# The rounded weights' buffers of feed-forward and gates start 128 bytes later

## The chip, the cores and the metric

The kernel runs on one core of one Trainium2 chip. The metric is the time of one execution on the device, in microseconds (us); lower is better. The core has four engines that compute: TensorE (PE in the rows; its weight loads are PEld), VectorE (DVE), ScalarE (ACT) and GpSimd (POOL). SP, the sync engine, issues most DMAs. An engine's work is in its own order; between engines, semaphores set the order.

## What is computed

512 tokens of width 1024 pass through two blocks in float32. The first has a Hyena mixer, neighbourhood attention, a pooling mixer and 16 experts of a mixture with a choice by the experts. The second has a gated delta rule and an mLSTM, and ends as follows; the change is in the memory that this end uses:

```python
mixed = jax.nn.sigmoid(gate_a) * y_a + jax.nn.sigmoid(gate_b) * y_b
x = x + mixed @ w_out
h = _rmsnorm(x, g_ffn)
x = x + (jax.nn.silu(h @ w1) * (h @ w3)) @ w2          # 1024 -> 2816 -> 1024
gate = jax.nn.sigmoid(_rmsnorm(x, g_ple) @ w_ple_gate)  # 1024 -> 1024
x = x + gate * (p_i @ w_ple)
return _rmsnorm(x, g_final)
```

## The kernel before

**Memory.** One tensor, the arena, holds 53200 words of 4 bytes in each of the 128 partitions. Places are given in words: `view(start, ...)` is a float32 view of it, and `rounded(name, start, n)` a tensor of the type fp32r laid over the same place. The ring of weight slots begins at word 11024: four slots (R) of 2048 words (WCH). B is 19216, T0 is 39696. Where a sentence says "slot i", it is `view(11024 + 2048 * i)`.

**Products in three parts.** A float32 product is made of three in fp32r: an operand is split into a rounded part (hi) and what rounding left (lo), and lo x hi, hi x lo and hi x hi are summed in PSUM. For weights this takes three steps: SP loads a chunk of 1 MB (128 x 2048 words) into a slot; ScalarE copies it, rounded, into `whi[i]` (lines 1773, 1808, 1819, 128x2048 each); VectorE subtracts that from the slot and writes the rest back over the slot itself, as `wlo[i]` (lines 1420, 1466, 1487). Then TensorE may read both. `whi[i]` is `weight_rounded{i}` in the rows, `wlo[i]` is `weight_rest`.

**The stages that use whi.** They are the last three, and TensorE runs them in this order:

- the up half of the feed-forward: 22 chunks, two for each pair of column tiles (w1 and w3), `up_tile`, lines 962 to 964. Of its three products for each of 8 steps, 962 has wlo as the stationary operand, 963 and 964 have whi. Each streams 512 columns of the tokens. In a row of TensorE the moving operand is named first and the stationary one second.
- the down half: 12 chunks, lines 993 to 995. Here the weights are the moving operand of 512 columns; 993 and 995 read whi. The hidden values' rounded part is made by ScalarE (line 1805), their rest by VectorE (line 1462), in the order 4 rests of hidden values, then the chunk's rest.
- the gates: 4 chunks, lines 1022 to 1024, in the same form; 1022 and 1024 read whi.

A slot is loaded anew when the products of the chunk four before have been made. Between the products TensorE turns tiles with an identity (line 548 for the norms' inputs, line 972 for the scale of the rows).

Before these, the projection units (lines 601 to 603) and the branch products (lines 929 to 931) work in the same way with other buffers for the rounded part: `unit_rounded` and `branch_rounded`. The two branch buffers lie at words 33552 and 35600 (lines 1724 and 1376 are their copy and difference).

**Places before.** whi[i] is at T0 + 4096 + 2048 i, that is word 43792 + 2048 i. The four end at T0 + 12288, where `junk` of 1024 words begins: squares for the norms are written there and never read; only their sum is used (lines 521, 1839, 1853, 1862).

Of the kernel before, what the change touches and what calls it, by code (L numbers as in the profile page):

```python
# [14 lines left out]
D = 1024  # L15
# [29 lines left out]
R = 4  # L45
LOW = 16
WCH = 2048
# [115 lines left out]
def program(nc, A, out):  # L163
    ctx = ExitStack()
    with ctx:
# [20 lines left out]
        def view(start, *dims):  # L186
            n = int(np.prod(dims))
            v = arena[:, start:start + n]
            if len(dims) == 2:
                v = v.rearrange("p (a b) -> p a b", b=dims[1])  # L190
            elif len(dims) == 3:
                v = v.rearrange("p (a b c) -> p a b c", b=dims[1], c=dims[2])
            return v

        def rounded(name, start, n):

            return nc.alloc_sbuf_tensor_at(name, [P, n], F32R, offset=arena_at + 4 * start)[:, :]
# [184 lines left out]
        T0 = B + 20480  # L382
# [41 lines left out]

        junk = view(T0 + 12288, D)
        blk = grow[:, 0:7 * P].rearrange("p (l c) -> p l c", c=P)
        maT = view(T0, 4, 512)
        atT = view(T0 + 2048, 4, 512)  # L430
# [44 lines left out]
        def qkv_unit(u):  # L475

            return u if u < U_GATES else u + 1
        whi = [rounded(f"weight_rounded{i}", T0 + 4096 + WCH * i, WCH) for i in range(R)]


        ahi = [rounded(f"hidden_rounded{k}", B + 512 * k if k < 8 else B + 13312 + 512 * k, L) for k in range(NFT)]
# [2960 lines left out]
```

How the kernel before makes its waits and increments, by code:

```python
            def wait(self, n=None):  # L399
                self.eng.wait_ge(S(self.name), self.n if n is None else n)
# [21 lines left out]
        def wait_chunk(pe, c):  # L422
            pe.wait_ge(S(f"chunk_in{c % R}"), 16 * (c // R + 1))
# [93 lines left out]
        def norm_square(act, norm, i, ready, n):  # L517
            act.wait_ge(S(ready), nth(ready, n))
            act.wait_ge(S("norm_sq"), NT * norm + i)
            act.activation(junk, x_res[:, i, :], ACT.Square, accum_out=nstat[norm][:, i:i + 1]).then_inc(S("norm_sq"), 1)
# [1 line left out]
        def norm_root(act, norm):  # L523
            act.wait_ge(S("norm_var"), NT * (norm + 1))
            act.activation(nstat[norm], nstat[norm], ACT.Sqrt).then_inc(S("norm_sd"), NT)
# [1 line left out]
        def norm_scales(dve, norm):  # L527
            dve.wait_ge(S("norm_sq"), NT * (norm + 1))
            dve.tensor_scalar(nstat[norm], nstat[norm], 1.0 / D, EPS, ALU.mult, ALU.add).then_inc(S("norm_var"), NT)
            dve.wait_ge(S("norm_sd"), NT * (norm + 1))
            dve.reciprocal(nstat[norm], nstat[norm]).then_inc(S("r_made"), 1)
# [1 line left out]
        def norm_var(dve, norm, i):  # L534
            dve.wait_ge(S("norm_sq"), NT * norm + i + 1)
            v = nstat[norm][:, i:i + 1]
            dve.tensor_scalar(v, v, 1.0 / D, EPS, ALU.mult, ALU.add).then_inc(S("norm_var"), 1)
# [1 line left out]
        def norm_rstd(dve, own, norm, i):  # L539
            dve.wait_ge(S("norm_sd"), NT * norm + i + 1)
            v = nstat[norm][:, i:i + 1]
            own(dve.reciprocal(v, v))
            own.wait()
```

## Time and profile before

| | us |
|---|---|
| median of 3 runs | 2056.72 |
| lowest and highest run | 2054.0, 2059.84 |
| span of the profiled execution | 2052.9 |
| TensorE busy in it | 1952.2 |
| VectorE busy | 730.4 |
| ScalarE busy | 532.1 |
| GpSimd busy | 118.6 |

The span runs from the first to the last instruction of one execution that the hardware profiler took. Busy time of TensorE is that of pipelined products: two overlap, so the duration of one is longer than the step from one start to the next, and the step is what the stage pays. The page's second part gives TensorE's granted clock as a share of its full 2.4 GHz; the lower level is half of it.

### The profile page before, as it was taken

To read this page: it belongs to the slowest core of one execution; us is meant where nothing else is said; L and a number is where in the kernel's file an instruction comes from. 1 tells how busy PE (TensorE), PEld (TensorE's weight loads), DVE (VectorE), ACT (ScalarE), POOL (GpSimd) and SP (SyncE) were. 2 spreads that over 40 slices of the span, in tenths; PEclk is the share of its full clock that TensorE was granted. 3 is DMA by queue.
4 is the path that set the end of the run, shared out by engine and by line. 5 is a ranking of instruction groups with operands and counts; after the bars stand their busy time and mean duration, and the time that the engine had idled before them with its cause. 6 is when DMAs were issued, how large, how long until landed. Compare 5 with 4: busy or idle time off the path is not lost.

```text
span 2052.9 us, 22852 instructions
## 1 busy us (share of the span) xinstructions
PE 1952.2 (95%) x9422; PEld 1211.6 (59%) x9422; DVE 730.4 (36%) x1069; ACT 532.1 (26%) x828; POOL 118.6 (6%) x127
## 2 busy tenths in 40 slices
PE   8999999989899897989899899999999999999998
PEld 6867843333333332323333368878888888888886
DVE  5648331101001010100101067595588443345225
ACT  5236220101000000101000056334444332234125
POOL 3432000000000000000000000141000000000000
PEclk9999999999999999999999999999999999999999
DMA  9420789999999999999999933212114222323331
GB/s 273 144 72 18 297 342 430 427 431 429 431 430 432 432 430 427 432 430 429 431 434 425 423 128 134 82 43 83 62 62 146 101 83 82 119 85 113 109 140 59
DMA packets 42295, 517.33 MB, mean 252 GB/s; under 512 B 5216, under 2 KB 5344, under 8 KB 12656
## 3 DMA queue, kind: packets, MB, share of 16 engines
q1 hardware_dynamic: 39728, 508.39, 60.6%
q0 software_dynamic: 2496, 7.92, 1.8%
q8 instruction: 53, 0.87, 0.2%
q14 instruction: 18, 0.15, 0.0%
HBM read 508.92 MB, written 6.29 MB: 251 GB/s over the span
## 4 chain that ended last, share of the span: by engine, by line
PE 73%; DMA 20%; DVE 5%; ACT 1%; issue 1%; POOL 0%; SPq 0%; ACTq 0%; DVEq 0%
DMA arena<-in_w_gu_dram 19%; PE bank L2517 15%; PE bank L2542 6%; PE bank L964 4%; PE bank L963 4%; PE bank L962 4%; PE bank L601 3%; PE bank L602 3%; PE bank L603 3%; PE bank L2479 2%; PE bank L994 2%; PE bank L993 2%; PE bank L995 2%; PE bank L2143 2%; PE bank L2149 2%; PE bank L2145 2%
## 5 line engine op out<-in xcount | busy, mean ns | idle before, releaser
L2517 PE MATMUL bank<-arena 128*64 128x512 f32 x2048 | 480.3, 625 | 67.8 <-DMA arena<-in_w_gu_dram 63.9
L2517 PEld LDWEIGHTS bank<-arena 128*64 128x64 f32 x2048 | 163.1, 143 | 360.2 <-issue 348.0
L3014 DVE TENSOR_TENSOR arena<-arena,bank 128x256 f32<-128x256 f32 x64 | 27.0, 421 | 639.6 <-ACT arena L3255 639.6
L2542 PE MATMUL bank<-arena 128*64 128x512 f32 x1024 | 232.6, 595 | 0.6 <-ACT arena L3259 0.6
L3255 ACT ACTIVATE arena<-bank 128x256 f32<-128x256 f32 x64 | 24.6, 384 | 537.0 <-PE bank L2517 537.0
L2542 PEld LDWEIGHTS bank<-arena 128*64 128x64 f32 x1024 | 73.7, 137 | 139.2 <-issue 139.2
L962 PE MATMUL bank<-input_rounded,weight_rest 128*128 128x512 f32 x352 | 137.2, 390 | 0.0
L964 PE MATMUL bank<-input_rounded,weight_rounded 128*128 128x512 f32 x352 | 137.0, 389 | 0.0
L963 PE MATMUL bank<-input_rest,weight_rounded 128*128 128x512 f32 x352 | 137.0, 389 | 0.0
L601 PE MATMUL bank<-input_rounded,weight_rest 128*128 128x512 f32 x312 | 125.9, 403 | 1.2 <-DVE weight_rest L1050 1.2
L603 PE MATMUL bank<-input_rounded,unit_rounded 128*128 128x512 f32 x312 | 122.4, 392 | 0.0
L602 PE MATMUL bank<-mix_rest,unit_rounded 128*128 128x512 f32 x312 | 122.3, 392 | 0.0
L3259 ACT ACTIVATE arena<-bank 128x256 f32<-128x256 f32 x64 | 24.6, 384 | 214.9 <-PE bank L2528 214.9
L963 PEld LDWEIGHTS bank<-input_rest,weight_rounded 128*128 128x128 f32 x352 | 66.1, 188 | 13.8
L962 PEld LDWEIGHTS bank<-input_rounded,weight_rest 128*128 128x128 f32 x352 | 66.1, 188 | 13.7
L964 PEld LDWEIGHTS bank<-input_rounded,weight_rounded 128*128 128x128 f32 x352 | 66.1, 188 | 13.6
L1420 DVE TENSOR_TENSOR weight_rest<-arena,weight_rounded 128x2048 fp32r<-128x2048 f32 x22 | 50.3, 2291 | 52.1 <-ACT weight_rounded L1773 51.9
L993 PE MATMUL bank<-weight_rounded,hidden_rest 128*128 128x512 f32 x176 | 68.8, 391 | 0.0
L995 PE MATMUL bank<-weight_rounded,hidden_rounded 128*128 128x512 f32 x176 | 68.5, 389 | 0.0
L994 PE MATMUL bank<-weight_rest,hidden_rounded 128*128 128x512 f32 x176 | 68.5, 389 | 0.0
L1553 ACT ACTIVATE unit_rounded<-arena 128x1024 fp32r<-128x1024 f32 x45 | 47.3, 1059 | 79.4 <-PE bank L603 63.8
L601 PEld LDWEIGHTS bank<-input_rounded,weight_rest 128*128 128x128 f32 x312 | 59.1, 189 | 14.7 <-DVE weight_rest L1050 1.6
(528 smaller groups left out, 2851.1 us busy)
## 6 DMA issues: line engine op xcount, KB each, us to landing
arena<-in_w_gu_dram SPq DMA_DIRECT2D x47, 4096.0 KB, 28.9
arena<-in_w_d_dram SPq DMA_DIRECT2D x62, 2048.0 KB, 26.5
arena<-in_wpack_dram SPq DMA_DIRECT2D x83, 1024.0 KB, 5.0
arena<-in_w_gu_dram SPq DMA_DIRECT2D x32, 2048.0 KB, 17.4
arena<-in_w_d_dram SPq DMA_DIRECT2D x4, 1024.0 KB, 10.0
arena<-in_w_gu_dram SPq DMA_DIRECT2D x3, 1024.0 KB, 8.3
arena<-in_xT_dram SPq DMA_DIRECT2D x4, 512.0 KB, 7.2
arena<-in_x_dram SPq DMA_DIRECT2D x2, 1024.0 KB, 13.2
```

The costliest lines, as they stand in the source:

```text
L601: mm(b, wl[:, k, :], hhi[k], start=k == 0, stop=False)
L602: mm(b, wh[:, k, :], chlo[k], start=False, stop=False)
L603: last = mm(b, wh[:, k, :], hhi[k], start=False, stop=k == KD - 1)
L962: mm(b, wl[:, k, m], hhi[k], start=k == 0, stop=False)
L963: mm(b, wh[:, k, m], hlo[k], start=False, stop=False)
L964: last = mm(b, wh[:, k, m], hhi[k], start=False, stop=k == KD - 1)
L993: mm(b, alo[k][:, t], wh[:, k - 4 * d, :], start=k == 0, stop=False)
L994: mm(b, ahi[k][:, t], wl[:, k - 4 * d, :], start=False, stop=False)
L995: last = mm(b, ahi[k][:, t], wh[:, k - 4 * d, :], start=False, stop=k == NFT - 1)
L1420: tt(out=wlo[(c + which) % R], in0=w, in1=whi[(c + which) % R], op=ALU.subtract)\
L2517: last = mm(ab[64 * x:64 * x + 64, :], xsT[:, k, 64 * x:64 * x + 64], w[x][k], start=k == 0, stop=k == KD - 1)
L2542: last = mm(bank[4 + n][64 * x:64 * x + 64, :], hidT[c % 2][:, P * t + 64 * x:P * t + 64 * x + 64], w[:, x, t, 512 * n:512 * n + 512], sta ...
```

## The change

The four buffers of rounded weights and the junk behind them start 32 words, 128 bytes, later. Sizes, instructions, waits and their order are as before. The 32 words ahead of whi[0] are used by nothing in these stages.

```diff
-        junk = view(T0 + 12288, D)
+        junk = view(T0 + 12288 + 32, D)
...
-        whi = [rounded(f"weight_rounded{i}", T0 + 4096 + WCH * i, WCH) for i in range(R)]
+        whi = [rounded(f"weight_rounded{i}", T0 + 4096 + 32 + WCH * i, WCH) for i in range(R)]
```

## Rows read from the trace of the kernel before

**Rows 1.** The page's head and its line of busy times.

```profile
span 2052.9 us, 22852 instructions
PE 1952.2 (95%) x9422; PEld 1211.6 (59%) x9422; DVE 730.4 (36%) x1069; ACT 532.1 (26%) x828; POOL 118.6 (6%) x127
```

**Rows 2.** Windows: from:to, length, busy us (count) of each engine, clock, DMA.

```profile
1637.00:2044.00 407.00, 407.00 (x1815) 336.96 (x1813) 168.00 (x171) 137.99 (x142) 0.00 (x0) 1.00 0.27 99
2044.00:2052.90 8.90, 0.00 (x0) 0.00 (x0) 4.32 (x10) 3.79 (x7) 1.40 (x1) 0.65 0.32 118
```

**Rows 3.** Timeline of PE, start and duration in us: up stage, then branch stage.

```profile
1701.98 0.39 PE L964 MATMUL bank<-input_rounded,weight_rounded 128*128 128x512 f32 x1
...
1705.38 0.39 PE L964 MATMUL bank<-input_rounded,weight_rounded 128*128 128x512 f32 x1
...
1600.05 0.39 PE L931 MATMUL bank<-branch_rounded,mixed_rounded 128*128 128x512 f32 x1
...
1603.45 0.39 PE L931 MATMUL bank<-branch_rounded,mixed_rounded 128*128 128x512 f32 x1
```

**Rows 4.** Timeline of PE behind a group of transposes in the up stage.

```profile
1648.01 0.60 PE L972 MATMUL bank<-arena 128*128 128x128 f32 x4
1648.36 0.48 PE L962 MATMUL bank<-input_rounded,weight_rest 128*128 128x512 f32 x1
1648.68 0.39 PE L963 MATMUL bank<-input_rest,weight_rounded 128*128 128x512 f32 x1
```

**Rows 5.** Chain that ended last: start, us, what; one piece of 16 transposes.

```profile
1969.61 1.75 PE bank L548 x16
```

**Rows 6.** Instructions by line: durations min/median/max in ns, first and last start.

```profile
L1773 ACT ACTIVATE weight_rounded<-arena x22: 1897/1918/1924, 1613.2 to 1841.1; 128x2048 fp32r<-128x2048 f32 x22
L1808 ACT ACTIVATE weight_rounded<-arena x12: 1905/1917/1926, 1860.3 to 1963.6; 128x2048 fp32r<-128x2048 f32 x12
L1420 DVE TENSOR_TENSOR weight_rest<-arena,weight_rounded x22: 2283/2292/2293, 1615.5 to 1843.1; 128x2048 fp32r<-128x2048 f32 x22
L1466 DVE TENSOR_TENSOR weight_rest<-arena,weight_rounded x12: 2281/2292/2294, 1862.3 to 1965.6; 128x2048 fp32r<-128x2048 f32 x12
L1724 ACT ACTIVATE branch_rounded<-arena x8: 1902/1917/1923, 1538.8 to 1611.4; 128x2048 fp32r<-128x2048 f32 x8
L1376 DVE TENSOR_TENSOR weight_rest<-arena,branch_rounded x8: 2286/2292/2293, 1540.8 to 1613.3; 128x2048 fp32r<-128x2048 f32 x8
```

**Rows 7.** Instructions by line, two others of VectorE.

```profile
L2692 DVE TENSOR_TENSOR arena<-bank,arena x2: 691/692/692, 99.7 to 105.1; 128x512 f32<-128x512 f32 x2
L2641 DVE TENSOR_TENSOR weight_rest<-arena,first_weight x20: 1215/1220/2104, 15.6 to 108.0; 128x1024 fp32r<-128x1024 f32 x20
```

**Rows 8.** Timeline at the second down chunk: its rest, its first product.

```profile
1880.91 2.29 DVE L1466 TENSOR_TENSOR weight_rest<-arena,weight_rounded 128x2048 fp32r<-128x2048 f32 x1
...
1887.84 0.39 PE L993 MATMUL bank<-weight_rounded,hidden_rest 128*128 128x512 f32 x1
```

**Rows 9.** The page's groups: count, then busy us, mean ns, idle before.

```profile
L962 PE MATMUL bank<-input_rounded,weight_rest 128*128 128x512 f32 x352 | 137.2, 390 | 0.0
L964 PE MATMUL bank<-input_rounded,weight_rounded 128*128 128x512 f32 x352 | 137.0, 389 | 0.0
L963 PE MATMUL bank<-input_rest,weight_rounded 128*128 128x512 f32 x352 | 137.0, 389 | 0.0
L601 PE MATMUL bank<-input_rounded,weight_rest 128*128 128x512 f32 x312 | 125.9, 403 | 1.2 <-DVE weight_rest L1050 1.2
L603 PE MATMUL bank<-input_rounded,unit_rounded 128*128 128x512 f32 x312 | 122.4, 392 | 0.0
L602 PE MATMUL bank<-mix_rest,unit_rounded 128*128 128x512 f32 x312 | 122.3, 392 | 0.0
...
L963 PEld LDWEIGHTS bank<-input_rest,weight_rounded 128*128 128x128 f32 x352 | 66.1, 188 | 13.8
```

**Rows 10.** Instructions by line: the tail's square into junk.

```profile
L1853 ACT ACTIVATE arena<-arena x1: 629/629/629, 2046.2 to 2046.2; 128x512 f32<-128x512 f32 x1
```

## The prediction

> **What bounds the kernel now.** Read the page first: one core, a span of 2052.9 us, TensorE busy for 95% of it [rows 1]. The edit touches only the end of the kernel, so the next view is the busy time of each engine in the stretch from 1637.0 us, where the first product with a moved buffer starts, to 2044.0 us, where the last one starts, and in the tail behind it [rows 2]. In the stretch TensorE is busy for 407.00 of 407.00 us at a granted clock of 1.00, its upper level of 2.4 GHz; VectorE has 168.00 us of work there, ScalarE 137.99, GpSimd none. TensorE alone is the bound.
>
> How close is it to its own floor? The timeline gives starts: line 964 at 1701.98 and again, 15 products later, at 1705.38, so 3.40 / 15 = 226.7 ns from one 128x128 by 512-column product to the next [rows 3]. The stretch has 22 x 2 x 3 x 8 = 1056 such products of the feed-forward's up half, 4 x 22 x 2 x 3 = 528 of the down half, and 8 x 8 x 3 = 192 of the gates: 1776. 1776 x 226.7 ns = 402.6 us. The other 36 instructions of the stretch's 1815 (three more began just before it) are transposes: 4 of line 972 and 32 of line 548. Sixteen of those take 1.75 us, 0.109 each [rows 5], so 36 take 3.9. They stand in six groups, and behind a group the pipe refills: the first product after line 972 starts at 1648.36 and the next at 1648.68, 0.32 us in place of 0.227, so some 0.1 us for each group, 0.6 in all [rows 4]. 402.6 + 3.9 + 0.6 = 407.1, against 407.0. Nothing is left over but rounding; I allow 1 us for what such a sum can hide.
>
> **The change part by part.** It adds, removes and reorders no instruction, wait or DMA; it changes start addresses. Four buffers of 8 KiB per partition (whi) and the throw-away output of the squares (junk) move up by 128 bytes. No instruction before 1613 us reads or writes them. Who touches them:
>
> (1) ScalarE writes whi from a ring slot: 38 copies of 128x2048. The median is 1918 or 1917 ns, from 1897 to 1926 in lines 1773 and 1808 [rows 6]. (2) VectorE reads slot and whi and writes the difference back over the slot: 38 of 2291 ns or so, between 2281 and 2294 in lines 1420 and 1466 [rows 6]. (3) TensorE reads whi in two of every three products: 704 + 352 + 128 = 1184, in the up half as the stationary operand, in the down half and the gates as the moving one. (4) ScalarE's squares write junk, one half-width square of them in the tail.
>
> Slot i and whi[i] lie 32768 words, exactly 128 KiB, apart now. If that distance cost something, another distance should be cheaper. The trace has one: the branch weights are rounded into buffers that start 88 KiB behind slot 0, so at other multiples of 8 KiB from their slots. The same copy takes 1917 there and the same difference 2292 ns (medians of lines 1724 and 1376) [rows 6]. So (1) and (2) have no penalty to lose that depends on this distance. For a step of 128 bytes itself the trace has no twin. The nearest are the two products of line 2692, on VectorE, which write 512 elements into rows 2176 bytes apart (an odd multiple of 128), at 691 and 692 ns, one like the other [rows 7]. I take zero for (1) and (2).
>
> What if it isn't zero? Both hide under TensorE, and the tightest place sets the cover. VectorE starts the rest of the second down chunk at 1880.91 and ends it 2.29 us later, at 1883.20; TensorE first reads it at 1887.84 [rows 8]. That leaves 4.6 us. The slowest that any such difference got in this trace is 2104 ns where 1215 is the least (line 2641) [rows 7]: a factor of 1.73, which would add 1.67 us to a 2.29 us difference. Even so TensorE wouldn't wait. In the other direction, a faster copy or difference ends earlier before the same 4.6 us, and buys nothing: ring slots come free by TensorE's products, not by VectorE.
>
> (3) is the only part on the path. 226.7 ns at 2.4 GHz are 544 cycles for 512 columns. If the 32 extra cycles came from reading whi beside the other operand, they should be missing where other buffers are read. They aren't: the branch stage has line 931 at 1600.05 and, 15 products on, at 1603.45, 226.7 ns again [rows 3]. That stage keeps its rounded weights at another place in the memory and at another distance from the stationary operand. I take zero for (3). Bounds: below, at most the 1 us above; above, the worst neighbour that I have, the projection units, where the three products have a mean of (125.9 + 122.4 + 122.3) / 936 = 395.9 ns where the up half has (137.2 + 137.0 + 137.0) / 1056 = 389.4 [rows 9]. That is 6.5 ns, true waits included, and is too high by those.
>
> (4) The tail's square of 512 elements is 629 ns [rows 10], on ScalarE, and sits beside or on the last chain. A change of a few per cent is 0.02 us. Zero.
>
> Sum: 0 on the path. The profiled span is 2052.9 us and the three runs have a median of 2056.72, 3.8 more, which I keep as what lies around the span. Forecast **2056.7 us**.
>
> Here a rule of the Trainium skill bears on the upper bound. The trace shows the copies, with DMA and other engines at work beside them, within 1897 to 1926 ns, which is not one fixed number [rows 6]. SBUF — State Buffer, section "Who interferes with whom", says that only the port pair shared by VectorE and GpSimd causes contention, and that TensorE and ScalarE never wait on anyone. By that the slower rival below is impossible and its time is that of the forecast; by the rows it stays open, with a small chance. The same page's section on the DMA port swizzle speaks against an effect of any such shift too: it puts the cost in 16-byte lines, of which 128 bytes are eight whole ones. No row here shows a line's cost.
>
> **The rivals.** (A) *The copies and differences change, hidden.* ScalarE or VectorE rows of whi move by tens of ns or more. For it: nothing but that the exact 128 KiB is gone. Against: the equal rows at another distance [rows 6]. Time the same, 2056.7, by the 4.6 us of cover.
>
> (B) *Slower: TensorE's read of whi.* Place: the 1184 products that read it. A new start makes the weight load or the moving stream meet another stream of reads or writes at the same place of the memory, and the product gets longer. Price: at the 6.5 ns of the units, 1184 x 6.5 = 7.7 us, so 2064.4. It decides above 0.3% (6.2 us), so from 6.2 / 1184 = 5.2 ns a product, 2.3% of 226.7. Against it: some 70 of the copies and differences run beside the stretch's products, and the sum for it leaves nothing over; weight loads are 188 ns of the 226.7 [rows 9] and so have 39 ns of room of their own.
>
> (C) *Faster: the 32 cycles are a conflict after all*, and go with the shift. 512 columns at 2.4 GHz would be 213.3 ns (estimate: one column a cycle), 13.4 less, x 1184 = 15.8 us, so 2040.9. Against: the same 226.7 in a stage that doesn't touch whi [rows 3].
>
> (D) *The change does nothing it says*, since where a tile starts has no part in any of these durations. That isn't apart in time from the forecast.
>
> **How the numbers follow.** About 0.3%, 6.2 us, is what a measurement of this kernel can tell from no change. Forecast (with D) 0.81, A 0.10, B 0.05, C 0.04. So within 0.3%: 0.91; slower by more: 0.05; faster by more: 0.04. The forecast's own spread isn't from the sum, whose end below is 1 us, but from one run to the next: the three runs span 2054.0 to 2059.84, 3 us to each side. I take 2052.5 to 2061.0, a little wider for another session. It leaves out B and C, and with the forecast's own tails some 0.15.
>
> **What would show it.** In the changed kernel's profile: line 964 to line 964 fifteen products on, 3.40 us; the stretch from the first line 962 to the last line 1024, 407 us; the copies of lines 1773 and 1808 at 1917 and the differences of 1420 and 1466 at 2292 ns. A differs in these copies only; B and C show as a start-to-start step away from 226.7 ns in lines 962 to 964, 993 to 995 and 1022 to 1024 and not in line 931. A span that moved with none of these means a difference outside the edit, in the 1637 us before it. The prediction is wrong if a step of 128 bytes matters where steps of 4 KiB and 8 KiB don't: that is the one thing that the rows can't exclude.

## The result and the profile after

| | before | after |
|---|---|---|
| median, us | 2058.41 (5 runs) | 2065.78 (5 runs) |
| lowest and highest, us | 2054.0, 2059.84 | 2062.47, 2066.5 |
| span of the profiled execution, us | 2052.9 | 2064.0 |

The ratio is 1.0039, 95% interval 1.0028 to 1.0050: slower by about 8 us. The forecast was no change, with a range that ended at 2061.0; both were wrong.

Where do the 8 us go? The first view is that of the three stages again, by windows from the first product of each stage to the first of the next (the last ends at the start of the last product). Columns as in rows 2. Before:

```profile
1637.01:1876.96 239.95, 239.95 (x1063) 198.71 (x1062) 96.62 (x96) 77.08 (x71) 0.00 (x0) 1.00 0.25 94
1876.96:1999.70 122.74, 122.74 (x557) 101.90 (x556) 49.09 (x45) 36.04 (x36) 0.00 (x0) 1.00 0.36 129
1999.70:2043.61 43.91, 43.91 (x199) 36.34 (x197) 21.90 (x31) 24.86 (x36) 0.00 (x0) 1.00 0.14 49
```

After:

```profile
1639.66:1886.55 246.89, 246.89 (x1063) 198.79 (x1062) 96.68 (x96) 77.20 (x71) 0.00 (x0) 1.00 0.25 91
1886.55:2010.46 123.91, 123.91 (x558) 101.83 (x556) 49.10 (x45) 35.87 (x36) 0.00 (x0) 1.00 0.36 128
2010.46:2054.73 44.27, 44.27 (x199) 36.30 (x197) 22.07 (x31) 24.85 (x36) 0.00 (x0) 1.00 0.13 48
```

Same counts, same clock of 1.00, the same work of VectorE and ScalarE, TensorE busy from end to end, and longer: up by 6.94 us, down by 1.17, gates by 0.36, together 406.60 to 415.07, that is 8.47 us. 8.47 / 2057 is 0.41%, beside 0.39% measured (0.28 to 0.50). The spans differ by 11.1, and the 2.65 us more are the later start of the first up product (1639.66 in place of 1637.01). Nothing moved is used by TensorE before that point, and in the runs below that leave the earlier stages as they were it starts anywhere from 1635.9 to 1640.8 us, whatever their time. I take it for the spread of one execution.

Next the timeline of TensorE in the up half of the changed kernel (start, duration in us), as in rows 3:

```profile
1700.12 0.40 PE L964 MATMUL bank<-input_rounded,weight_rounded 128*128 128x512 f32 x1
1700.35 0.40 PE L962 MATMUL bank<-input_rounded,weight_rest 128*128 128x512 f32 x1
1700.59 0.39 PE L963 MATMUL bank<-input_rest,weight_rounded 128*128 128x512 f32 x1
1700.82 0.40 PE L964 MATMUL bank<-input_rounded,weight_rounded 128*128 128x512 f32 x1
...
1703.62 0.40 PE L964 MATMUL bank<-input_rounded,weight_rounded 128*128 128x512 f32 x1
```

From 1700.12 to 1703.62 are 15 products: 3.50 / 15 = 233.3 ns where it was 226.7 [rows 3]. All three lines are slow. The step behind 962 is 235 ns, behind 963 and 964 about 232.5. Of the stage's 350 triples that I could time, 344 take 0.700 us, so the copies of ScalarE, which run beside some of them, make no difference. In the down half the step behind 993 is the long one (232.4); behind 994 it is 226.2, behind 995 228.4 (means over the stage's starts in the timeline; before, each line's mean was 226.4 to 227.0 in the two halves). The branch stage isn't touched: line 931 starts at 1602.69 and, 15 products on, at 1606.10, 3.41 us.

What the prediction expected of the other engines holds. The copy and the difference are as in rows 6 (min/median/max ns):

```profile
L1773 ACT ACTIVATE weight_rounded<-arena x22: 1898/1917/1922, 1615.8 to 1849.3; 128x2048 fp32r<-128x2048 f32 x22
L1420 DVE TENSOR_TENSOR weight_rest<-arena,weight_rounded x22: 2284/2293/2295, 1618.2 to 1851.3; 128x2048 fp32r<-128x2048 f32 x22
```

And the page says which of TensorE's two kinds of instruction got longer:

```profile
L962 PE MATMUL bank<-input_rounded,weight_rest 128*128 128x512 f32 x352 | 140.0, 398 | 0.0
L964 PE MATMUL bank<-input_rounded,weight_rounded 128*128 128x512 f32 x352 | 139.0, 395 | 0.0
L963 PE MATMUL bank<-input_rest,weight_rounded 128*128 128x512 f32 x352 | 138.3, 393 | 0.0
...
L963 PEld LDWEIGHTS bank<-input_rest,weight_rounded 128*128 128x128 f32 x352 | 66.2, 188 | 15.6
```

Against rows 9 the products went from 389 or 390 ns to 393 to 398; the weight loads stayed at 188. Which load runs beside which product, the timeline of the loads shows:

```profile
1700.35 0.19 PEld L963 LDWEIGHTS bank<-input_rest,weight_rounded 128*128 128x128 f32 x1
1700.59 0.19 PEld L964 LDWEIGHTS bank<-input_rounded,weight_rounded 128*128 128x128 f32 x1
```

Line 962's product starts at 1700.35 too, and 963's at 1700.59: beside each product the weights of the next one are loaded.

### The profile page after: what moved, and what is told of

It reads as the page before. It is cut to its first block, busy times and chain, and to the rows that moved or that the text cites. A ratio compares the mean times of both kernels' runs of the same rounds, so it can differ in the third digit from the quotient of the medians.

```text
span 2064.0 us, 22852 instructions
## 1 busy us (share of the span) xinstructions
PE 1962.6 (95%) x9422; PEld 1214.4 (59%) x9422; DVE 730.4 (35%) x1069; ACT 531.9 (26%) x828; POOL 117.9 (6%) x127
## 4 chain that ended last, share of the span: by engine, by line
PE 72%; DMA 21%; DVE 5%; ACT 1%; issue 1%; SPq 0%; ACTq 0%; DVEq 0%
DMA arena<-in_w_gu_dram 20%; PE bank L2517 14%; PE bank L2542 6%; PE bank L962 4%; PE bank L964 4%; PE bank L963 4%; PE bank L601 3%; PE bank L602 3%; PE bank L603 3%; PE bank L2479 2%; PE bank L993 2%; PE bank L995 2%; PE bank L994 2%; PE bank L2143 1%; PE bank L2149 1%; PE bank L2145 1%
## 5 line engine op out<-in xcount | busy, mean ns | idle before, releaser
L2542 PE MATMUL bank<-arena 128*64 128x512 f32 x1024 | 232.5, 595 | 0.6 <-ACT arena L3259 0.6
L1420 DVE TENSOR_TENSOR weight_rest<-arena,weight_rounded 128x2048 fp32r<-128x2048 f32 x22 | 50.3, 2292 | 51.3 <-ACT weight_rounded L1773 51.1
```

What stands on the lines that cost most here:

```text
L1420: tt(out=wlo[(c + which) % R], in0=w, in1=whi[(c + which) % R], op=ALU.subtract)\
L2542: last = mm(bank[4 + n][64 * x:64 * x + 64, :], hidT[c % 2][:, P * t + 64 * x:P * t + 64 * x + 64], w[:, x, t, 512 * n:512 * n + 512], sta ...
```

## The experiments

The theory from here on: TensorE reads the moving operand of one product while it loads stationary weights for a product, and the two reads get in each other's way unless their operands start at the same place modulo some small stride (R). The rivals: ScalarE's and VectorE's accesses to whi are in the way (M); the place of whi in itself counts, its alignment (A); the distance between the two weight tiles wlo and whi counts (W). A step is the time from one start to the next; where one number stands for a stage, it is the mean. Single runs of a kernel differ by some 6 us (before: 2054.0 to 2059.84), so one run's time says little here. The lengths of the three stages say more: in three kernels that cost nothing they agree within 0.01 us.

**One shift for each buffer.** Buffer i serves each fourth chunk, so one kernel holds four shifts.

```diff
-whi = [rounded(f"weight_rounded{i}", T0 + 4096 + WCH * i, WCH) for i in range(R)]
+whi = [rounded(f"weight_rounded{i}", T0 + 4096 + [8, 16, 64, 128][i] + WCH * i, WCH) for i in range(R)]
```

(junk follows the last one, here and in all kernels below.)

> The four buffers of rounded weights begin 32, 64, 256 and 512 bytes later than before (8, 16, 64, 128 words), one shift for each buffer. In the changed kernel the up half's products came at 233.3 ns (three in 700 ns) where they had come at 226.7, and the first of the down half's three at 232.5. Theory R (relation): the cost depends on the distance between whi and another operand of TensorE, modulo some small stride. Then chunks in whi[0] to whi[3] have different steps, and those of the whole stride (512 bytes at the latest, since blocks of one tile lie 512 bytes apart and all cost the same before) are back at 226.7. Theory M (memory, other engines): ScalarE's and VectorE's accesses to whi disturb TensorE at any place but the old one: steps above 226.7 and irregular in time for all four. I expect 226.7 for whi[3] and 230 to 235 for at least two of the others.

> Shifts of 128, 384, 640 and 768 bytes (32, 96, 160, 192 words). whi[0] repeats the changed kernel: 233.3 ns in the up half, 232.5 for the first of three in the down half. Theory R with a stride of 512 bytes: whi[2] (640 = 512 + 128) equals whi[0]; with a stride of 256 bytes, whi[3] (768) is back at 226.7 too and whi[1] (384) equals whi[0]. Theory M: all four alike.

Single runs: 2062.53 and 2062.59 us beside 2059.5 for before. The three stages take 411.77 and 413.41 us, where before has 406.60. In the first of the two, line 964 in a part of the up half that uses whi[0] and then whi[1], and in one that uses whi[2] and then whi[3]:

```profile
1700.03 0.39 PE L964 MATMUL bank<-input_rounded,weight_rounded 128*128 128x512 f32 x1
...
1703.52 0.40 PE L964 MATMUL bank<-input_rounded,weight_rounded 128*128 128x512 f32 x1
...
1711.12 0.39 PE L964 MATMUL bank<-input_rounded,weight_rounded 128*128 128x512 f32 x1
...
1714.52 0.39 PE L964 MATMUL bank<-input_rounded,weight_rounded 128*128 128x512 f32 x1
```

15 products take 3.49 us at shifts of 32 and 64 bytes, and 3.40 at 256 and 512. In the second kernel 128, 384 and 640 bytes give 233.3 to 233.5 ns in the up half, all alike, and 768 bytes 226.8. So the cost repeats with 256 bytes, and a whole 256 bytes costs nothing. I had been sure of that for 512 bytes only. M falls: at three other places (256, 512 and 768 bytes) there is no cost.

**Move the ring and all above it.** The nine places with the ring's start, 11024, become 11056:

```diff
-        wring = [view(11024 + WCH * s, WCH) for s in range(R)]
-        B = 11024 + WCH * R
+        wring = [view(11056 + WCH * s, WCH) for s in range(R)]
+        B = 11056 + WCH * R
```

> Everything from the weight ring upwards begins 128 bytes later: slots, whi, hidden values, gates' low operands. whi keeps its old distance to the slots; what lies below the ring (the tokens' rounded parts hhi and the gates' ghi and glo 0 to 3, x) stays. If the distance between whi and wlo sets the step, up, down and gates are at 226.7 ns. If the distance between weights and the streamed tokens does, the up half, which streams hhi from below the ring, is slow (233 ns) and the down half, all of whose operands moved together, is at 226.7. If the place itself does (whi off a multiple of 256 or 512 bytes), both are slow and so are stages before.

2072.75 us beside 2059.5. Up is slow, at 232.5, 225.8 and 228.3 ns behind lines 962, 963 and 964; down is at 226.8. That fits R: 963 streams hlo, which moved with the weights, and 962 and 964 stream hhi, which stayed, and both are longer than before, if not equally. The same shift made earlier stages slow for the first time. In the first projection the weights moved and the tokens didn't; the timeline merges eight products a row:

```profile
66.96 2.02 PE L2145 MATMUL bank<-first_rest,first_weight 128*128 128x512 f32 x8
68.82 2.02 PE L2149 MATMUL bank<-input_rounded,weight_rest 128*128 128x512 f32 x8
```

From 66.96 to 68.82 are 8 products, 232.5 ns each; before, the steps behind these two lines had a mean of 226.7. The branch stage, which the prediction had compared with, is slow here as well: its weights moved and its rounded tokens (`mixed_rounded`, the stationary operand of two of its products) did not, and its steps have a mean of 233.3 ns. W falls: wlo and whi keep their distance, and the stages are slow.

**Move everything.** 32 words are put ahead of the arena.

```diff
-        arena = ctx.enter_context(nc.sbuf_tensor("arena", [P, 53200], F32))
+        ctx.enter_context(nc.sbuf_tensor("ahead", [P, 32], F32))
+        arena = ctx.enter_context(nc.sbuf_tensor("arena", [P, 53168], F32))
```

> The whole arena begins 128 bytes later, so that all distances are as before and all places are moved by 128 bytes. Theory R: 226.7 ns in every stage, the time of before (2056 us). If the place itself counts: 233 ns in up, and slower stages everywhere, 15 us or more in all.

2056.76 us beside 2059.5. The three stages by windows, as for before:

```profile
1639.12:1879.07 239.95, 239.95 (x1064) 198.73 (x1062) 96.64 (x96) 77.06 (x71) 0.00 (x0) 1.00 0.25 94
1879.07:2001.81 122.74, 122.74 (x558) 101.91 (x556) 49.08 (x45) 36.03 (x36) 0.00 (x0) 1.00 0.37 129
2001.81:2045.72 43.91, 43.91 (x199) 36.33 (x197) 21.92 (x31) 24.85 (x36) 0.00 (x0) 1.00 0.13 49
```

They are those of before to 0.01 us. A falls: whi lies 128 bytes later here too and costs nothing, since all lies later.

**The other shifts within 256 bytes.**

```diff
-whi = [rounded(f"weight_rounded{i}", T0 + 4096 + WCH * i, WCH) for i in range(R)]
+whi = [rounded(f"weight_rounded{i}", T0 + 4096 + [24, 40, 48, 56][i] + WCH * i, WCH) for i in range(R)]
```

> Shifts of 96, 160, 192 and 224 bytes (24, 40, 48, 56 words) for whi[0] to whi[3]. So far multiples of 256 bytes cost nothing, and 32, 64 and 128 bytes (mod 256) cost 4 to 8 ns a product in the up half. If TensorE's two streams of reads, the loads of the stationary operand and the moving operand, collide in a memory that repeats every 256 bytes, the cost has a shape over the 256 bytes. A distance that avoids a collision left over at 0 would show as a step below 226.7 ns, down to 213 (512 columns at 2.4 GHz). I expect none below 226.5, and 229 to 236 for all four.

2065.53 us beside 2057.87. With the runs above this gives the eight shifts within 256 bytes in steps of 32 bytes. Mean step of the three lines, in ns:

| shift modulo 256 bytes | up half | down half |
|---|---|---|
| 0 (before; 256, 512, 768) | 226.7 to 227.2 | 226.7 to 227.5 |
| 32 | 231.7 | 233.3 |
| 64 | 232.3 | 231.2 |
| 96 | 230.8 | 232.2 |
| 128 (also 384, 640) | 233.3 to 233.5 | 228.9 to 229.1 |
| 160 | 232.0 | 232.5 |
| 192 | 229.6 | 234.4 |
| 224 | 233.4 | 232.8 |

None is below the 226.7 ns of before, so no place tried for whi beats the old one. 128 bytes is the mildest shift for the down half and among the worst for the up half.

**Which load meets the stream?** In both kernels whi is 128 bytes later, and some moving operands of the up half are replaced by a piece of whi, `wm`. What they add to the sums has no meaning.

```diff
+                    wm = whi[(c + which) % R].rearrange("p (q n) -> p q n", n=512)
...
-                        mm(b, wh[:, k, m], hlo[k], start=False, stop=False)
-                        last = mm(b, wh[:, k, m], hhi[k], start=False, stop=k == KD - 1)
+                        mm(b, wh[:, k, m], wm[:, k % 4, :], start=False, stop=False)
+                        last = mm(b, wh[:, k, m], wm[:, k % 4, :], start=False, stop=k == KD - 1)
```

> whi 128 bytes later as in the changed kernel. In the up half the moving operands of lines 964 and 965 (963 and 964 before) are now a piece of 512 columns of whi itself, so that stationary and moving operand of each product start at the same place modulo 256 bytes: (wlo, tokens), (whi, whi), (whi, whi). The sums of the up half are wrong by that. Only the load that runs beside a product, that of the next one, still differs for two of three. If the collision is between a moving operand and the load of the next product's weights, the up half stays at 228 to 233 ns. If it is between a moving operand and its own weights, it is back at 226.7.

```diff
+                    wm = whi[(c + which) % R].rearrange("p (q n) -> p q n", n=512)
...
-                        mm(b, wl[:, k, m], hhi[k], start=k == 0, stop=False)
-                        mm(b, wh[:, k, m], hlo[k], start=False, stop=False)
+                        mm(b, wl[:, k, m], wm[:, k % 4, :], start=k == 0, stop=False)
+                        mm(b, wh[:, k, m], wm[:, k % 4, :], start=False, stop=False)
```

> The opposite: whi 128 bytes later, and moving operands (whi, whi, tokens) with the weights (wlo, whi, whi) in the up half, which leaves its sums wrong. Now each moving operand starts at the same place modulo 256 bytes as the weights loaded beside it, those of the next product, and differs from its own weights in two of three. If the load that runs beside counts: 226.7 ns. If the own weights count: 228 to 233.

Single runs: 2061.63 and 2060.78 us beside 2057.87. The steps behind the three products are 230.8, 234.2 and 228.3 ns in the first, 230.0, 230.0 and 233.3 in the second: 13.3 ns a triple above 680 in both, where the changed kernel has 20. Neither theory holds alone. The stage is slow where all products agree with their own weights and two disagree with the load beside them, and it is slow where that is turned round. The single steps don't fit either theory: the product in the middle, line 963 of before, agrees with both in both kernels, and the steps behind it are 234.2 and 230.0 ns. The pair also lacks a control: no run has these replaced operands with whi at its old place, so whether the replacement costs something by itself isn't shown. Which of TensorE's reads meet, and how that leads to just these numbers, stays open.

**A whole 256 bytes, and the up half alone.** These two have 11 and 10 runs, beside 21 of before.

```diff
-whi = [rounded(f"weight_rounded{i}", T0 + 4096 + WCH * i, WCH) for i in range(R)]
+whi = [rounded(f"weight_rounded{i}", T0 + 4096 + [64, 64, 64, 64][i] + WCH * i, WCH) for i in range(R)]
```

> The change with 256 bytes in place of 128: all four buffers and junk 64 words later. If only the place modulo 256 bytes counts, the ratio to before is 1.000 (0.999 to 1.001), and the three stages are at 226.7 ns. If any other move of whi costs something (its order behind other buffers, the junk), it is 1.002 or more.

Ratio 1.0001 (0.9992 to 1.0010), and the three stages together take what they took before (window of the stages):

```profile
1640.83:2047.44 406.61, 406.61 (x1815) 336.88 (x1813) 167.61 (x171) 137.94 (x142) 0.00 (x0) 1.00 0.27 100
```

For the second, the up half gets tiles of its own, each 128 bytes from that of the down half and gates and over mostly the same words (lines 953, 1420 and 1773, by the numbers of before, use them):

```diff
-whi = [rounded(f"weight_rounded{i}", T0 + 4096 + WCH * i, WCH) for i in range(R)]
+whi = [rounded(f"weight_rounded{i}", T0 + 4096 + (0, 2112, 4160, 6272)[i], WCH) for i in range(R)]
+whi_up = [rounded(f"weight_rounded_up{i}", T0 + 4096 + (32, 2080, 4192, 6240)[i], WCH) for i in range(R)]
```

> The up half alone uses places that are 128 bytes (mod 256) off; down half and gates use places that are not. From the traces the up half lost 1056 x 6.6 ns = 6.9 us, the down half 1.2 and the gates 0.4. So the ratio should be 1.0034 (1.0025 to 1.0043), with 233 ns in the up half and 226.7 in the others. If the loss is somewhere else (before 1637 us), it stays near 1.000.

Ratio 1.0030 (1.0021 to 1.0040), with steps of 235.0, 232.8 and 232.2 ns in the up half and about 227 in down and gates. The stages take 246.90, 122.75 and 43.90 us: the up half has lost its 6.95, the others nothing. So the greater part of the change's 8.5 us lies in the up half, by the measured times too.

## Why the prediction was wrong

- **The bound** was read right. TensorE alone bounds the last 407 us, and what the products lost came out in the time: 8.47 us in the stages (0.41%), 0.39% in the runs.
- **Parts (1), (2), (4)**: zero, and zero was measured. The copies and differences keep medians of 1917 and 2292 or 2293 ns, as in rows 6, and the tail's square of 512 elements is 629 ns again, so rival A fell too. The 4.6 us of cover were never needed.
- **Part (3)** is the step that failed. It took zero for TensorE's reads of whi, and 8.47 us were measured, 6.94 in the up half and 1.53 in down and gates. The zero came from the equal 226.7 ns of the branch stage at another distance [rows 3]. But that distance, like all those between TensorE's large operands in this kernel, is a multiple of 256 bytes. The comparison varied the one thing that costs nothing. The prediction named this hole itself (a step of 128 bytes where only steps of KiB were seen) and gave it 0.05. With no row on either side, that was far too sure. With the ring moved by 128 bytes the branch stage itself went to 233.3 ns.
- **Rival B** was what happened: right engine, right stages, right sign. That its price came so near, 7.7 us against 8.47, was luck. The 6.5 ns were a difference of durations, waits included, in the projection units; from start to start the units' products are 227.4 to 227.9 ns apart in the mean in the trace of before, 1 ns from the up half's. And its count was off in both directions. All 1056 products of the up half got longer, by 6.6 ns on average, also those of line 962, which read wlo and run beside a load from whi; the down half and gates lost 1.53 us on 720 products, 2.1 ns each.
- **The reasons against B** didn't bear. That the sum of the stretch leaves nothing over says that nothing comes on top of 226.7 ns a product at the old distances, and nothing of new ones. And the 39 ns between a load's 188 and the step of 226.7 are no room: it is the product that got longer (393 to 398 ns from 389 or 390), while the load stayed at 188 [rows 9].
- **Rival C** asked whether the 32 cycles above 512 columns are such a collision. At eight places within 256 bytes the mean step never fell below 226.7 ns, so C fell for every place tried; what the 32 cycles are stays open.
- **The rule of the Trainium skill** that would have excluded B, SBUF — State Buffer, section "Who interferes with whom", doesn't hold here. It says that TensorE's two read ports are independent and that it never waits on anyone. For the other engines the trace agrees: 344 of 350 triples take 0.700 us, whatever ScalarE and VectorE do beside them. For TensorE itself it disagrees: 226.7 ns became 233.3 when its own operands were moved against each other. The measurement decides. The section on the DMA port swizzle in the same page of the Trainium skill tells of 16-byte lines; that 128 bytes are eight whole ones didn't keep them from costing those 6.6 ns.

## What to carry to other kernels

Where TensorE bounds and streams its operands from the on-chip memory, place all stationary and moving operands of a stage a whole number of 256 bytes apart. Here a shift by 256 bytes cost nothing, and one of 32 to 224 bytes cost 1 to 3% of the mean step. That is shown for fp32r products of 128x128 by 512 columns; other types and shapes weren't tried. Padding or shifting one buffer by anything else should be costed as a change to every product that reads it and to their neighbours. And when a prediction rests on "other distances cost the same", write down what all the distances seen have in common before you put a small chance on the new one.

## What the runs showed of the hardware that I had not expected

- The step of a product of 128x128 by 512 columns in fp32r at a granted clock of 1.00 was 226.7 to 227.5 ns, as a mean over a stage or over one buffer's part of it, where all moving and stationary operands start at the same place modulo 256 bytes, and 229 to 234 ns where whi doesn't (up to 237.8 for a single line's).
- It is the relation that counts: with everything 128 bytes later, the three stages took 406.60 us, as before.
- The cost reaches products whose own two operands agree (235 ns behind line 962 in the changed kernel), and it doesn't add up singly. With two of three products off their own weights a triple lost 6.9 ns in the changed kernel's down half, and 6.6 in the up half with the ring moved, where wlo and whi are off alike. It lost 20 in the changed kernel's up half, and as much in the branch stage with the ring moved; in both, the stationary operand changes its place modulo 256 bytes within a triple. With every product off its own weights, the first projection lost 5.8 ns a product.
- ScalarE's and VectorE's instructions don't show it: with the copy's destination and the difference's second source 128 bytes off, the medians stayed at 1917 and 2292 or 2293 ns.
